# A hybrid decoder step on one core: the transposes of a quarter move in front of the last values of the quarter before

## What is computed

```python
def fox_attend(q, fq, pq, k, v, fk, pk):
    s = jnp.einsum('bqhd,bkhd->bhqk', q, k).astype(jnp.float32) * (HEAD_DIM ** -0.5)
    s = s + jnp.swapaxes(fq, 1, 2)[..., :, None] - jnp.swapaxes(fk, 1, 2)[..., None, :]
    s = jnp.where(pq[:, None] >= pk[None, :], s, -jnp.inf)
    p = jax.nn.softmax(s, axis=-1)
    return jnp.einsum('bhqk,bkhd->bqhd', p.astype(v.dtype), v)
```

## Time and profile before

| | us |
|---|---|
| three runs | 694.05, 696.24, 697.59 (median 696.24) |
| the profiled execution: time | 691.88 |
| its span | 690.3 |
| mean granted clock | 0.999 of full speed |
| TensorE busy | 653.8 (95% of the span) |
| VectorE, ScalarE, GpSimd busy | 391.0, 259.8, 150.6 |

### The profile page before, as it was taken

How to read it: one execution, slowest core, us unless ns; L and a number is a source line. 1 busy time by engine, 2 the same in 40 slices (tenths; PEclk the granted TensorE clock), 3 DMA queues, 4 the chain that set the end, 5 groups by cost and what they waited for, 6 DMA issues and landing times.

```text
span 690.3 us, 13168 instructions
## 1 busy us (share of the span) xinstructions
PE 653.8 (95%) x5145; PEld 562.0 (81%) x5145; DVE 391.0 (57%) x712; ACT 259.8 (38%) x479; POOL 150.6 (22%) x167
## 2 busy tenths in 40 slices
PE   4899999999999999999999989999999889999996
PEld 3889999898999889999999965766667655688884
DVE  5743926673455315159999967335443458654543
ACT  6537343111111245221112063745564557332321
POOL 3554112111111011223312040123222201121210
PEclk9999999999999999999999999999999999999999
DMA  8412103131100032344120282567666533123132
GB/s 229 144 43 62 32 1 75 32 92 31 32 11 23 5 84 80 83 159 123 30 62 1 82 254 88 159 168 218 182 199 191 171 140 107 41 67 122 61 123 91
DMA packets 59735, 67.29 MB, mean 97 GB/s; under 512 B 14156, under 2 KB 49883, under 8 KB 59673
## 3 DMA queue, kind: packets, MB, share of 16 engines
q1 hardware_dynamic: 54505, 51.37, 25.1%
q0 software_dynamic: 5168, 15.08, 7.4%
HBM read 57.71 MB, written 8.68 MB: 96 GB/s over the span
## 4 chain that ended last, share of the span: by engine, by line
PE 83%; DVE 8%; ACT 5%; issue 2%; POOL 1%; DMA 1%; SPq 0%; DVEq 0%; ACTq 0%; POOLq 0%
PE PS L1872 14%; PE PS L1873 13%; PE PS L1874 13%; PE PS L1775 4%; PE PS L1776 4%; PE PS L1777 4%; PE PS L2159 3%; PE PS L2141 3%; PE PS L2094 3%; PE PS L2116 2%; PE PS L2059 2%; PE PS L2046 2%; DVE rows_odd L1654 2%; DVE YF L1533 1%; PE PS L2185 1%
## 5 line engine op out<-in xcount | busy, mean ns | idle before, releaser
L1872 PE MATMUL PS<-xh,wh 128*128 128x368 f32 x576 | 196.3, 341 | 0.8 <-POOL wl L628 0.5
L1873 PE MATMUL PS<-xl,wh 128*128 128x368 f32 x576 | 190.3, 330 | 0.0
L1874 PE MATMUL PS<-xh,wl 128*128 128x368 f32 x576 | 189.9, 330 | 0.0
L628 POOL TENSOR_TENSOR wl<-wr,wh 128x1024 fp32r<-128x1024 f32 x24 | 61.7, 2570 | 262.9 <-ACT wh L1003 262.9
L1872 PEld LDWEIGHTS PS<-xh,wh 128*128 128x128 f32 x576 | 108.3, 188 | 4.9 <-issue 1.5
L1873 PEld LDWEIGHTS PS<-xl,wh 128*128 128x128 f32 x576 | 108.3, 188 | 0.9
L1874 PEld LDWEIGHTS PS<-xh,wl 128*128 128x128 f32 x576 | 108.3, 188 | 0.0
L609 DVE TENSOR_TENSOR wr<-wr,small 128x1024 f32<-128x1024 f32 x24 | 35.4, 1477 | 41.1 <-DMA wr<-in_w_in_dram 41.0
L1513 DVE RECIPROCAL RA<-RA 128x1104 f32<-128x1104 f32 x8 | 56.4, 7053 | 0.3
L1775 PE MATMUL PS<-woh,yh 128*128 128x512 f32 x128 | 50.6, 395 | 0.0
L1777 PE MATMUL PS<-woh,yl 128*128 128x512 f32 x128 | 50.3, 393 | 0.0
(11 more groups left out here) (325 smaller groups left out, 1118.4 us busy)
## 6 DMA issues: line engine op xcount, KB each, us to landing
wr<-in_w_in_dram SPq DMA_DIRECT2D x24, 512.0 KB, 3.8
kpage<-in_cache_fox_k_dram SPq DMA_DIRECT2D x64, 192.0 KB, 2.7
RA<-in_cache_fox_v_dram POOLq DMA_DIRECT2D x32, 192.0 KB, 3.5
pagesB<-in_cache_fox_v_dram POOLq DMA_DIRECT2D x32, 192.0 KB, 3.8
YF<-in_x_prompt_dram SPq DMA_DIRECT2D x8, 512.0 KB, 5.8
xres<-in_x_prompt_dram SPq DMA_DIRECT2D x8, 512.0 KB, 3.8
out_y_p_dram<-zout SPq DMA_DIRECT2D x16, 256.0 KB, 2.1
wo_raw_a<-in_w_out_dram SPq DMA_DIRECT2D x6, 512.0 KB, 5.0
```

The costliest lines, as they stand in the source:

```text
L628: eng.tensor_tensor(low, wr[:, c % 2, :, 0:m], wh[:, c % 2, :, 0:m].bitcast(F32), ALU.subtract).then_inc(wlo_done, 1)
L1872: pe.matmul(out, high, xh[:, k, cols], start=(k == 0), stop=False)
L1873: pe.matmul(out, high, xl[:, k, cols], start=False, stop=False)
L1874: ins = pe.matmul(out, low, xh[:, k, cols], start=False, stop=(k == KT - 1))
```

## The change

It is in `plan()`. The values left over from the quarter before, and its sum, are no longer appended at the head of a quarter, except for the quarters 1 and 11 (counted from 0), which are (0,1) and (2,3). In the other nine, (0,2) to (2,2), they are appended behind the new quarter's first two transposes:

```diff
-        if behind:
+        if n_q in (1, len(QUARTERS) - 1):
             order += [("V", unit) for unit in behind] + [("R", ("sum",) + behind[0][:2])]
-        behind = []
+            behind = []
         ahead = scored(*QUARTERS[n_q + 1]) if 0 < n_q < len(QUARTERS) - 1 else []
@@ -208,6 +208,8 @@
                     order.append(("I", (p, q)))
             order += BEHIND_TURNS.get(units[first], [])
             order += [("V", unit) for unit in behind]
+            if first == 0 and behind:
+                order.append(("R", ("sum",) + behind[0][:2]))
             behind = units[first:last]
```

## The result

| | before | changed |
|---|---|---|
| median of 20 runs, us | 694.17 | 695.74 |
| lowest to highest | 691.13 to 697.59 | 694.80 to 699.91 |
| profiled execution: time, span | 691.88, 690.3 | 695.05, 693.4 |

The ratio is 1.0036, with a 95% interval of 1.0021 to 1.0052: slower, clear of no change, and inside the 0.5% that I had called indistinguishable. It is not the quotient of the two medians, which is 1.0023 and lies inside the interval as well. The profiled execution took 695.05 us, where I had forecast 694.9 for it; the median is 695.74, where I had forecast 699.3, with a range of 697.6 to 700.8. The three runs shown before the prediction had a median 2 us above that of the twenty.

A forecast was written before the change was run, and what follows sets the result against it. TensorE's queue and the holes in it were taken to bound the stage; 4 x 0 + 2 x 1.2 + 0.65 + 2 x 0 = 3.05 us on 696.24 gave 699.3 us, own range 697.6 to 700.8, widened to 695.5 to 702.0.

The forecast's parts named there:

- The two borders into last quarters: Borders into the fourth quarters of the first two head pairs: second page transpose 1.2 us late each, 2.4 us together.
- the chain: At last-quarter borders: transposes, values, VectorE's waiting copy, two multiplications, then a free bank at 447.55 instead of 446.34.
- (2,2): Border into the last pair's third quarter: transposes wait for exponentials, first row maximum 0.65 us late, bounds -0.24 and +0.85.
- The four borders with ScalarE's exponential: Borders into first and third quarters with cache work ahead: the exponential holds the copy, scores start as before; 0 each.
- smaller by the moved work or gone in name: Expected sign at the first-quarter borders: the wait before the scores shrinks or vanishes, yet scores start no earlier.
- The two second-quarter borders: Second quarters of the second and third pairs: VectorE decides, row maxima 0.13 us later against a small gain; 0 each.
- Rival 3: Multiplications push the first row maximum at seven borders, 0.85 us each, beside 2.4 us at last quarters: 704.5 us; chance 0.11.
- rival 1: At the last-quarter borders the sum's bank is free in time, only (2,2) pays 0.65 us: 696.9 us; chance 0.14.
- rival 2: TensorE's waits on ScalarE's copy before the scores go, -3.6 us: 692.7 us, 0.5% faster; chance 0.05.
- (1,0): Border into the second pair's first quarter: scores wait 1.04 us on ScalarE's copy, forecast to start as before; value 0.
- within: Verdict that the whole kernel's time change stays inside 0.5%, 3.5 us; given 0.68, slower 0.29, faster 0.03.
- The starting time: Whole kernel before the change: median 696.24 us of three runs (694.05 to 697.59), to which 3.05 us was added.

The follow-up runs named there:

- e2: New order only at the two borders into last quarters, all others as in the kernel before: ratio to before 1.0034, stage +2.76 us.
- e4: Changed kernel, but at the last-quarter borders VectorE does its two multiplications ahead of the second transposes' copy: ratio to before 1.0035, stage 195.71 us.
- e5: New order at the six borders forecast at 0, others as before, ScalarE's copy ahead of its sample exponential: ratio to before 0.9948, stage 191.70 us.
- e1: New order only at the six borders forecast at 0; last-quarter borders and (2,2) as in the kernel before: ratio to before 0.9996.
- e3: New order only at (2,2), all other borders as in the kernel before: ratio to before 1.0002.
- e8: At all nine changed borders only the first of two transposes goes ahead of last values and sum: ratio to before 1.0018, stage 196.18 us.
- e6: Kernel before, but both transposes ahead of the sample's scores at the first-quarter borders of the second and third pairs: ratio 0.9956, stage 192.06 us.
- e7: As e6, with transposes, values and sum also ahead of the sample's scores at the two second-quarter borders: ratio to before 0.9956, stage 190.93 us.
- e9: As e7, plus the new order with ScalarE's copy before its exponential at the two third-quarter borders: ratio to before 0.9933, stage 190.32 us.

## Why the prediction was right where it was, and where it was not

- **The two borders into last quarters** (forecast 1.2 us each, measured 1.35 and 1.36): the chain was right link by link. From the start of the values to the page transposes the trace has 444.06 to 447.40, 3.34 us; the forecast had 444.21 to 447.55, the same 3.34. e2 shows these borders alone, e4 that VectorE's order is 0.97 of them. The missing 0.15 lies ahead of and behind the chain: the interrupted transposes took 1.95 us instead of 1.87, and the page transposes, once stopped, 0.49 us to the next row instead of 0.44.
- **(2,2)** (0.65; measured 0.61 in its piece and 0.66 at the first row maximum): right, with the stop at 0.64 us, where I had named 0.8. Likewise the wait at the page transposes is listed with 0.87 us, where I had named 1.1.
- **The four borders with ScalarE's exponential** (0; measured 0.00 to 0.02): right, and e5 shows the reason. But what I said would show it, a wait "smaller by the moved work or gone in name", contradicts my own reasoning: with the same matmuls in front of the scores and the same copy end the wait must stay 1.04 us, and it did.
- **The two second-quarter borders** (0; measured 0.06 and -0.01): right. VectorE carries the multiplications there now, and TensorE's two small waits became one of 0.79 us in front of the third scores.
- **Sum:** 3.05 us forecast, 3.41 in the stage, 3.1 in the span, since the changed profile's stage began 0.24 us sooner; the ratio says 2.5 us (1.5 to 3.6). Rival 3 (the row maxima pushed at all seven borders; its sum is 704.6, not 704.5) is refuted by e1, rival 1 (the bank free in time) by the 0.87 us wait, rival 2 (the holes close) by (1,0).
- **What failed is not the chain of waits but its two ends: the step from microseconds to a verdict, and the time that the sum starts from.** The prediction put "what can be told from no change here" at 0.5% and with it 0.68 on "within". The measurement told 0.36% apart from none, with 0.16% on either side. A forecast of +0.44% from a chain of rows that left no way out, with one clear sign, should have been called "slower". The bound of 3.5 us is as wide as the spread of the three single runs, 694.05 to 697.59, and a median over twenty is surer than that.
- **The starting time, 696.24 us, was the mis-sized term of the sum.** The forecast of 699.3 was 3.6 us too high, and the measured 695.74 lies below its own range of 697.6 to 700.8. Of the 3.6 us 2.1 are the starting median (696.24 of three runs, 694.17 of twenty), the rest is the difference between 3.05 and the 1.57 by which the medians differ. With the median of twenty the sum would have given 697.2. A single run of before lies anywhere from 691.13 to 697.59, and the range of the forecast had left too little room for that.

## What to carry to other kernels

Work moved from ahead of a hole into it closes the hole only if what ends the hole comes sooner by the move. Here ScalarE's copy did not, TensorE had the same work ahead of the scores, and the 1.04 us stayed. So look at what the releasing engine did in the microsecond before, and move that (here its exponential: 2.55 us of the stage, 0.4%) instead of the waiting engine's work. When items are reordered in a list that several engines share, write down each engine's new order and follow every buffer that the moved items hold: here two short multiplications behind a copy held one of three banks, and cost more than all the rest. A wait on the way that nobody felt before is the price of a cover taken away; if the rows show each link, trust the sum's sign even where it is small.

## What the runs showed of the hardware

**The clock fell behind two short waits, in two profiles.** e1 and e3 have 1.2 us more in the piece of (1,0), with the new order in the one and the old in the other. The table of stretches of e1, with the granted clock as the third number from the right, shows a stretch at 0.66, which is part of it at the lower of the two levels, 1.2 instead of 2.4 GHz:

```profile
465.00:467.50 2.50, 1.46 (x13) 0.76 (x12) 0.77 (x3) 1.04 (x3) 1.26 (x3) 1.00 0.76 238
467.50:472.50 5.00, 4.34 (x27) 3.54 (x25) 3.00 (x17) 1.24 (x3) 2.45 (x5) 0.66 0.68 193
```

The timeline of e1 has what TensorE did before it:

```profile
466.09 0.94 PE L2118 MATMUL PS<-YF 64*128 64x400 f32 x4 [1.04 <-ACT PT L1252]
...
468.32 1.23 PE L2118 MATMUL PS<-YF 64*128 64x256 f32 x4 [0.66 <-DVE pmax L1656]
```

Behind waits of 1.04 and 0.66 us, 2.2 us apart, the same scores take 1.23 us instead of 0.70. Two of the seven profiles with both waits (in e8 the first is 0.89 us) had this at (1,0), none at (2,0), and none of the four (e5, e6, e7, e9) in which the first wait was gone. Two of seven against none of four can be chance: that the waits bring the fall about, or that shorter ones prevent it, is not shown.

The clock fell elsewhere too. In the stretches of e5, e7, e8 and e9 it was low twice in the input projection, which the edits do not touch: at about 27 us, and again between 165 and 175 (e5, e8) or 240 and 250 us. The second of e7 came with no wait of TensorE listed from 200 us on, and TensorE busy for 5.00 of 5.00 us:

```profile
240.00:245.00 5.00, 5.00 (x25) 4.40 (x24) 1.54 (x3) 4.98 (x6) 0.34 (x1) 0.63 0.02 3
```

These are the four profiles with the lowest mean clocks, 0.991 to 0.993, and in them the second stage starts 1.5 to 4.2 us later than in the profile of before; but in e1, e3 and e4, which have no such fall, it starts 1.1 to 1.4 us later as well. What brings these falls about is open.

**Times follow the mean clock.** The runs' mean granted clock lies between 0.987 and 0.999. Of the 29 runs of before beside e5 to e8, 12 had 0.998 or more, with a median of 692.20 us; all 29 have 694.32. Taken at 0.998 and more alone, e5 is at 689.82 (7 of 9 runs), e6 at 690.37 (9 of 9), e7 at 689.34 (6 of 12): 2.4, 1.8 and 2.9 us below before, near the stages' 2.6, 2.2 and 3.3, while the ratios ask for 3.6, 3.1 and 3.1. In the runs of e5 to e8 the part of the ratio that no stage shows goes with the clock; where in the program each of these runs lost it is known for the profiled ones alone.
